# Two attention layers of a four-layer kernel, reordered as a two-step software pipeline

## The reference

```python
def nsa_attention(h, ...):                    # layer 3, 16 heads of 64 in 4 groups
    o_cmp = ...   # attention to 15 compressed blocks of 32 keys (a small MLP makes them)
    s_sel = einsum('bcgrd,bgckd->bcgrk', qc, kg) * scale + bias     # selected keys
    o_sel = softmax(s_sel) @ vg
    o_win = banded_attention(q, kwn, vwn, WIN - 1, 1, rel_bias)     # window of 256
    return (g0 * o_cmp + g1 * o_sel + g2 * o_win).reshape(B, S, D_MODEL) @ w_out

def dilated_attention(h, w_q, k_shared, v_shared, w_out, rel_bias): # layer 4
    q = (h @ w_q).reshape(B, S, N_DIL, N_KV, GQA_R, HEAD_DIM)       # 3 dilations
    for gi, (window, dilation) in enumerate(DILATIONS): ...         # (128,1) (512,4) (2048,16)
    o = sum over dilations of o_i * softmax(lse)_i                  # one joint softmax
    return o.reshape(B, S, D_MODEL) @ w_out
```

## Time and profile before

| | us |
|---|---|
| median of 3 runs | 1893.71 (1890.61 to 1898.06) |
| profiled execution | 1888.3, of which the span is 1886.5 |
| layer 3, from its first scores to the next stage's first matmul | 1104.25 to 1249.82 |
| layer 4, the same | 1516.11 to 1666.05 |
| TensorE in the span | busy 95%, mean granted clock 0.967 |

### The profile page before, as it was taken

How to read it: one execution, slowest core, us unless ns; L and a number is a source line. 1 busy time by engine, 2 the same in 40 slices (tenths; PEclk the granted TensorE clock), 3 DMA queues, 4 the chain that set the end, 5 groups by cost and what they waited for, 6 DMA issues and landing times.

```text
span 1886.5 us, 31683 instructions
## 1 busy us (share of the span) xinstructions
PE 1794.1 (95%) x13416; PEld 1684.9 (89%) x13416; DVE 1222.6 (65%) x1918; ACT 935.6 (50%) x1280; POOL 124.1 (7%) x35
## 2 busy tenths in 40 slices
PE   7999999999999999999999978799999988889998
PEld 6999999999889999999998877569998977779996
DVE  6976766877569767668775657556554734456453
ACT  5446565544355465655443546445443654445442
POOL 2612000000017120000000000000000000000000
PEclk9899999999999999999999999789999998899999
DMA  8684445555546644455555462224555645225552
GB/s 235 163 235 147 149 157 186 167 183 179 202 140 188 192 144 148 157 191 166 180 179 205 135 181 91 90 67 157 179 201 194 182 139 134 90 90 184 185 211 79
DMA packets 249148, 305.75 MB, mean 162 GB/s; under 512 B 9778, under 2 KB 224142, under 8 KB 249007
## 3 DMA queue, kind: packets, MB, share of 16 engines
q1 hardware_dynamic: 235959, 289.66, 47.7%
q10 hardware_dynamic: 13048, 14.07, 3.5%
HBM read 299.51 MB, written 4.19 MB: 161 GB/s over the span
## 4 chain that ended last, share of the span: by engine, by line
PE 76%; DVE 10%; DMA 6%; ACT 5%; issue 2%; DVEq 1%; ACTq 0%; SPq 0%
PE psum L463 23%; PE psum L464 23%; PE psum L465 23%; DVE wlo L439 3%; DMA raw<-in_b_w_q 2%; ACT whi L431 2%; DMA raw<-in_w_ffn_gate 2%; PE psum L2385 1%; DMA raw<-in_a_w_in 1%; DMA raw<-in_b_w_out 1%; ACT work L2018 1%; DVE work L2246 1%; DMA x<-in_x 1%; DMA raw<-in_a_w_out 1%; DVE hT L617 0%
## 5 line engine op out<-in xcount | busy, mean ns | idle before, releaser
L431 ACT ACTIVATE whi<-raw 128x2048 fp32r<-128x2048 f32 (+2 forms) x277 | 526.6, 1903 | 552.3 <-PE psum L465 177.6
L439 DVE TENSOR_TENSOR wlo<-raw,whi 128x2048 fp32r<-128x2048 f32 x249 | 563.3, 2281 | 183.3 <-PE psum L465 158.7
L463 PE MATMUL psum<-hT,whi 128*128 128x256 f32 x2160 | 616.9, 286 | 7.5 <-DVE wlo L439 3.8
L464 PE MATMUL psum<-hT,whi 128*128 128x256 f32 x2160 | 613.0, 284 | 0.0
L465 PE MATMUL psum<-hT,wlo 128*128 128x256 f32 x2160 | 612.9, 284 | 0.0
L463 PEld LDWEIGHTS psum<-hT,whi 128*128 128x128 f32 x2160 | 416.4, 193 | 10.9 <-issue 5.5
L464 PEld LDWEIGHTS psum<-hT,whi 128*128 128x128 f32 x2160 | 416.5, 193 | 0.1
L465 PEld LDWEIGHTS psum<-hT,wlo 128*128 128x128 f32 x2160 | 416.2, 193 | 0.0
L439 POOL TENSOR_TENSOR wlo<-raw,whi 128x2048 fp32r<-128x2048 f32 (+1 forms) x28 | 122.8, 4390 | 585.6 <-ACT whi L431 402.7
L463 PE MATMUL psum<-whi,hT 128*128 128x256 f32 (+2 forms) x448 | 145.1, 324 | 1.1 <-issue 1.1
L465 PE MATMUL psum<-whi,hT 128*128 128x256 f32 (+2 forms) x448 | 144.3, 322 | 0.0
(11 more groups left out here) (352 smaller groups left out, 2832.0 us busy)
## 6 DMA issues: line engine op xcount, KB each, us to landing
raw<-in_w_in SPq DMA_DIRECT2D x78, 1024.0 KB, 5.7
raw<-in_ffn_w_up SPq DMA_DIRECT2D x44, 1024.0 KB, 5.2
raw<-in_w_ffn_gate SPq DMA_DIRECT2D x22, 1024.0 KB, 5.4
raw<-in_w_ffn_up SPq DMA_DIRECT2D x22, 1024.0 KB, 6.4
raw<-in_w_ffn_down SPq DMA_DIRECT2D x22, 1024.0 KB, 5.0
raw<-in_ffn_w_down SPq DMA_DIRECT2D x22, 1024.0 KB, 5.2
raw<-in_b_w_q SPq DMA_DIRECT2D x12, 1024.0 KB, 5.7
raw<-in_a_w_in SPq DMA_DIRECT2D x10, 1024.0 KB, 5.8
```

The source lines that it names most:

```text
L431: act.activation(part(whi, n, HIGH_SLOTS), part(raw, n, RAW_SLOTS), ACT.Copy).then_inc(high_made, 1)
L439: eng.tensor_tensor(part(wlo, n, LOW_SLOTS), part(raw, n, RAW_SLOTS), part(whi, n, HIGH_SLOTS).bitcast(F32), ALU.subtract).then_inc(stream ...
L463: nc.tensor.matmul(dst, left[0], right[0], start=first, stop=False)
L464: nc.tensor.matmul(dst, left[0], right[1], start=False, stop=False)
```

## The change

Both loops are turned into a pipeline of two steps:

- TensorE issues `scores(s+1)` before `context(s-1)` and `turn(s)`, and waits with it for the maxima of step s (`maxima_ready`), no longer for the copies.
- The transposes have banks of their own: 6 and 7 in layer 3, one for each head. In layer 4 they are cut into pieces of up to 4 blocks (an even step 3 pieces, an odd one 2), which take banks 5 and 7 in turn; a piece waits for the copy of the piece before last.
- VectorE weighs step s and then finds the maxima of s+1, and does its other work after that. ScalarE does `exps(s)` and then `copies(s-1)`. Probabilities and sums are held twice.
- Layer 3 has only banks 4 and 5 left for context, so groups 0 and 1 are copied out (`take_group`), their compressed part goes to a bank of its own and is added (`sum_group`). Layer 4 has bank 6 left, of which VectorE copies each finished half out (`take_context`), and bank 4 for dense products.
- The table `FILL` places the dense halves. In layer 3 evictions and `make_high` come at other steps. In layer 4 `evict` stands at steps 4g and 4g+1 behind `copies(s-1)`, and at 4g+3 ahead of it; the steps of `make_lows` in the code are the same numbers.

```diff
-            FILL = {0: ((6, 0), (6, 1)), 1: ((7, 0), None), 2: ((7, 1), (8, 0)), 3: ((8, 1), None), 4: ((9, 0), None),
-                    5: ((9, 1), (10, 0)), 6: ((11, 0), None), 7: ((12, 0), (13, 0)), 8: ((14, 0), None), 9: ((14, 1), None)}
...
+            FILL = {0: ((6, 0), (6, 1)), 1: ((7, 0), (7, 1)), 2: ((8, 0), (8, 1)), 3: ((9, 0), None), 4: ((9, 1), None),
+                    5: ((10, 0), None), 6: ((11, 0), None), 7: ((12, 0), None), 8: ((13, 0), None), 9: ((14, 0), (14, 1))}
...
+                        if s:
+                            pe.wait_ge(turned_copied.sem, turned_copied.at(2 * s + e - 1))
...
+                scores(0)
                 for s in range(STEPS):
-                    scores(s)
                     fill(s, 0)
+                    if s + 1 < STEPS:
+                        scores(s + 1)
...
-                    copies(s)
-                    if s == 0:
+                    if s:
+                        copies(s - 1)
+                    if s == 1:
                         evict(6)
+                    if s == 2:
+                        evict(7)
...
+                        evict(9)
                         block_high(1)
-                        make_high(act, n0 + 10 + HIGH_SLOTS + 1)
-                    if s == 6:
-                        make_high(act, n0 + 11 + HIGH_SLOTS + 1)
+                    if s in (6, 7, 8, 9):
+                        make_high(act, n0 + s + 4 + HIGH_SLOTS + 1)
...
-                        make_high(act, n0 + 13 + HIGH_SLOTS + 1)
-                    if s == 8:
+                        take_group(0)
...
+                    if s == 10:
+                        evict(14)
...
-                    if s == 12:
+                    if s == 13:
...
+                def sum_group(g):
+                    p = GROUP_BLOCKS[g]
+                    dve.wait_ge(bank_full.sem, bank_full.at(p + 1))
+                    dve.wait_ge(group_taken.sem, group_taken.at(g + 1))
+                    dve.tensor_tensor(part[:, g, :], own(p), part[:, g, :], ALU.add).then_inc(group_summed.sem, 1)
+
+                maxima(0)
+                for s in range(STEPS):
+                    weigh(s)
+                    if s + 1 < STEPS:
+                        maxima(s + 1)
...
+            FILL = {}
+            for g in range(QUADS - 1):
+                a, b, c = ([(LEAD + ND * g + i, j) for j in range(2)] for i in range(ND))
+                FILL[4 * g - 1], FILL[4 * g] = (None, None, a[0]), (a[1], None, b[0])
+                FILL[4 * g + 1], FILL[4 * g + 2] = (b[1], None, c[0]), (None, c[1], None)
...
+            def turns(s):
+                _, t, _, _ = step(s)
+                if t:
+                    return (((0, 0), (0, 1), (0, 2), (0, 3)), ((0, 4), (0, 5), (1, 0), (1, 1)),
+                            ((1, 2), (1, 3), (1, 4), (1, 5)))
+                return ((0, 0), (0, 1), (0, 2)), ((1, 0), (1, 1), (1, 2))
...
+            def turn_bank(m):
+                return bank((5, 7)[m % 2])
...
             def own(n):
-                return bank(4 + n % 2)
+                return bank(4 + n % 2) if n < LEAD else bank(4)
...
-                            pe.wait_ge(bank_free.sem, bank_free.at(n - 1))
+                            pe.wait_ge(bank_free.sem, bank_free.at(n if n >= LEAD else n - 1))
...
-                        pe.wait_ge(turned_copied.sem, turned_copied.at(2 * s))
+                        pe.wait_ge(maxima_ready.sem, maxima_ready.at(2 * s))
...
+                    for m, blocks in enumerate(turns(s), turns_until(s)):
+                        if m >= 2:
+                            pe.wait_ge(turned_copied.sem, turned_copied.at(m - 1))
+                        pe.wait_ge(probs_ready.sem, probs_ready.at(2 * s + blocks[-1][0] + 1))
+                        for i, (e, n) in enumerate(blocks):
+                            mm = nc.tensor.transpose(turn_bank(m)[:, i * P:(i + 1) * P],
+                                                     probs[:, 2 * (s % 2) + e, n * P:(n + 1) * P], ident)
                         mm.then_inc(probs_turned.sem, 1)
...
-                    pe.wait_ge(turned_copied.sem, turned_copied.at(2 * s + 2))
-                    if t and j >= 2:
-                        pe.wait_ge(parts_ready.sem, parts_ready.at(j - 1))
-                    b = bank(6 + j % 2)
+                    pe.wait_ge(turned_copied.sem, turned_copied.at(turns_until(s + 1)))
+                    if t and j:
+                        pe.wait_ge(context_taken.sem, context_taken.at(j))
+                    b = bank(6)[:, (j % 2) * S:(j % 2 + 1) * S]
...
+                scores(0)
+                fill(-1, 2)
                 for s in range(STEPS):
-                    scores(s)
-                    if i < 2 * count:
-                        dense_half(i)
-                        i += 1
+                    fill(s, 0)
+                    if s + 1 < STEPS:
+                        scores(s + 1)
+                    fill(s, 1)
                     if s:
                         context(s - 1)
                     turn(s)
-                    if s % 2 == 0 and i < 2 * count:
-                        dense_half(i)
-                        i += 1
+                    fill(s, 2)
...
                 def copies(s):
-                    _, _, _, blocks = step(s)
-                    for e in range(2):
-                        act.wait_ge(probs_turned.sem, probs_turned.at(2 * s + e + 1))
-                        act.activation(sbuf_t[:, 2 * (s % 2) + e, 0:blocks * P], slot(e)[:, 0:blocks * P], ACT.Copy) \
+                    for m, blocks in enumerate(turns(s), turns_until(s)):
+                        e, n = blocks[0]
+                        at, wide = 768 * e + n * P, len(blocks) * P
+                        act.wait_ge(probs_turned.sem, probs_turned.at(m + 1))
+                        act.activation(turned_probs[s % 2][:, at:at + wide], turn_bank(m)[:, 0:wide], ACT.Copy) \
                            .then_inc(turned_copied.sem, 1)
...
                     exps(s)
-                    if u < count and i >= 2:
-                        evict(u + i - 1)
-                    if s and s % 2 == 0:
-                        high(s // 2 - 1)
-                    copies(s)
-                    if u < count and i == 0:
-                        evict(u)
+                    if u < count and i == 3:
+                        evict(u + 2)
+                    if s:
+                        copies(s - 1)
+                    if u < count and i < 2:
+                        evict(u + i)
+                    if s >= 4 and s % 2 == 0:
+                        high(s // 2 - 2)
+                copies(STEPS - 1)
+                high(STEPS // 2 - 2)
                 high(STEPS // 2 - 1)
...
+                def take_context(j):
+                    dve.wait_ge(context_ready.sem, context_ready.at(j + 1))
+                    dve.tensor_copy(context_rows[:, j % 2, :], bank(6)[:, (j % 2) * S:(j % 2 + 1) * S]) \
+                       .then_inc(context_taken.sem, 1)
...
+                    weigh(s)
+                    if s + 1 < STEPS:
+                        maxima(s + 1)
                     if s and s % 2 == 0:
-                        low(s // 2 - 1)
+                        take_context(s // 2 - 1)
                     if s % 4 < 3:
                         make_lows(dve, n0 + min(LEAD + ND * (s // 4) + s % 4 + 2, count + 2))
+                    if s >= 4 and s % 2 == 0:
+                        low(s // 2 - 2)
+                low(STEPS // 2 - 2)
                 low(STEPS // 2 - 1)
```

More of the change, by code:

```diff
@@ L1939, in context @@
                     g = j // 2
-                    b = bank(4 + g)[:, (j % 2) * S + t * P:(j % 2) * S + (t + 1) * P]
+                    if g >= 2 and s % 4 == 0:
+                        pe.wait_ge(group_taken.sem, group_taken.at(g - 1))
+                    b = bank(4 + g % 2)[:, (j % 2) * S + t * P:(j % 2) * S + (t + 1) * P]
+                    last = g < 2 and s % 4 == 3
                     for n in range(2 * (t + 1)):
@@ L1970, in _ @@
                         turn_blocks(0)
-                    if s == 15:
-                        block_context(0)
-                        block_context(1)
+                block_context(0)
+                block_context(1)
                 context(STEPS - 1)
@@ L2228, in _, with maxima @@
                 dve.wait_ge(table_load.sem, table_load.at(16 * (P // ROWS + 2)))
-                for s in range(STEPS):
+                def maxima(s):
                     j, t, keys = step(s)
@@ L2287, in _ @@
                             block_weights(t_)
+                for g in range(2):
+                    sum_group(g)
                 for c in range(GROUPS):
                     dve.wait_ge(context_read.sem, context_read.at(c + 1))
-                    dve.tensor_tensor(hT[1][:, 2 * c:2 * c + 2, :].rearrange("p a s -> p (a s)"), bank(4 + c),
+                    dve.tensor_tensor(hT[1][:, 2 * c:2 * c + 2, :].rearrange("p a s -> p (a s)"),
```

(32 more changed lines are left out.)

185 lines of the change are left out of this document (113 added, 72 removed).

## The result

The changed kernel takes 1917.52 us (median of 4 runs, 1914.46 to 1923.52) against 1892.16 us (1887.38 to 1898.06, 4 runs, those shown ahead among them). The ratio is 1.0136, 95% interval 1.0098 to 1.0175. The profiled execution has a span of 1916.0 us, 29.5 more than before.

The account below looks back on a forecast made before the run. In layer 3 TensorE and VectorE, both loaded, wait for each other in turn; layer 4's middle rounds have little left to win. Layer 3 -25 and layer 4 +50 give +25 on the 1893.71 median: 1918 us, range 1885 to 1936.

Parts of the forecast that it names:

- Layer 3, -25: Layer 3 loop: scores no longer wait for the copies, 25 us saved, bounds -33 to -18.
- The cut parts: Layer 3's stretch to step 10 and its tail: 79 in place of 96.6 us, 37.5 in place of 48.97.
- Layer 4, +50: Layer 4 loop: a chain through all engines with bare loads makes it 50 us longer.
- the walk: Layer 4 chain priced leg by leg from the trace: 23.9, 20.9 and 12.2 us, +52 over the loop.
- The rounds: Layer 4's groups of four steps: first +16.6 us, next two +22.2 and +21.3, last -8.
- Stalls of third pieces: Layer 4, TensorE: transposes of an even step's third piece wait about 10 us for copies, twice a round.
- Load 5.1 us, nine bare: Layer 4: nine weight loads of 5.1 us each, from low part to split, covered by no other work.
- The clock: Layer 4, TensorE: half clock after two 10 us stalls costs 4.5 us a round; +40 without clock losses.
- The ring: Layer 4: low part, load, split, exponentials, copies and third piece wait on each other, 57.0 us a round at full clock.
- The rival that the loads are half hidden: Layer 4: loads end early or low parts come early, each of 9 legs loses 3 us; 1874 to 1894, chance 0.14.
- The other two: Pipeline works in both loops, 1854 us, chance 0.08; layer 3 gives back only 10, 1934 us, chance 0.12.
- rounds 2 and 3: Layer 4's two middle groups of four steps, 39.25 and 40.19 us before, said to have little left to win.

Follow-up runs that it names:

- both cuts: Two runs on the changed kernel: layer 4 low parts made a step or two earlier, 1844.28 us; layer 4 splits run a step later, behind the copies, 1853.95 us.
- the dose of half a load: Changed kernel with nine layer 4 weight loads bringing only half their unit (0.5 MB): 1909.48 us against 1921.94.
- early low parts: Layer 4 low parts made a step or more earlier: on the changed kernel 1844.28 us; on changed layer 3 with old layer 4, 1853.99 us.
- the longer filling: Changed kernel with 88 and 74 transposes of a constant ahead of third pieces in layer 4's three rounds: 1911.22 us.

## Why the prediction came out

The predicted 1918 us is 0.5 us from the median. The mechanism came out as walked, but so small a distance is luck. The two loops together grew by 31.5 us where +25 was forecast. Against that, 2 us less lie ahead of layer 3, and the kernel before was profiled in an execution 4 us below its median (1888.3 against 1892.16), while the changed one's profile (1917.9) lies at its median. Point by point:

- **Layer 3, -25**: -23.7. The cut parts came out at 80.6 us (79 walked) and 41.2 (37.5 walked, and 4 for the clock, which is at 0.79 there; no run prices that part). VectorE's waits ahead of the even maxima fell only from 22.0 to 14.9 us, where I had said under 8; of these 7.1 lie ahead of the first maxima, where the kernel before waits about as long (7.8; the one trace puts this wait down to a transfer, the other to the scores). Its waits for exponentials fell by 13.7 us (17.5 to 3.8), which the prediction did not count apart. The transposes' waits fell as said.
- **Layer 4, +50**: +55.2, against the +52 of the walk, which was rounded down. The rounds walked as 58.4, 61.5 and 61.5 took 59.6, 61.0 and 61.3; the last, walked as 21, took 23.3. Stalls of third pieces: 8.3 to 11.2 us, where 10 was said. The clock of the rounds is 0.77 to 0.81, under the 0.85 named.
- **Load 5.1 us, nine bare**: eight of the nine are between 4.8 and 5.2 us, one 6.4. The Trainium skill ("DMA: Bandwidth & Descriptors", section Measured) gives 6.15 us for 1 MB, measured on transfers issued from GpSimd; as an estimate the loop would be 9 us longer by it, and the trace does not have them.
- **The clock**: the walk has 2.3, 4.5 and 4.5 us in the three rounds, 11.3 in all; 10 to 12 measured. The rule of the Trainium skill that a loop whose waits idle TensorE falls back to the slow clock at each turn ("TensorE: Matmul & The Clock Gate", section "HAM oscillation — how this bites in real kernels") agrees with these rows: all six third pieces of the changed kernel came at half clock.
- **The ring as cause**: shown by both cuts and by the dose of half a load.
- The rival that the loads are half hidden was refuted by the 77.5 us of waits; VectorE had its spare time, but behind the waits. The other two fell with the loops, at -23.7 and +55.2 us.

What was missing in the prediction: it set the banks aside and gave their order no price. Of the 60.3 us of waits at the pieces, 46.5 go with the loads, and 13.8 stay. It did not see that moving three lines would open the ring. And it held that rounds 2 and 3 had little left to win: for the pipeline that is so (1.9 and 1.1 us over the old order, both with early low parts), but against the kernel before early low parts and pipeline together took 4.8 and 6.3 us off them (34.4 and 33.9 us in place of 39.3 and 40.2).

## What to carry to other kernels

When a pipeline gets one step deeper, list for each buffer which step gives it free and which step needs it full: here the activations moved a step apart, while the weights' low part, load and split stayed in one step, and the deeper order closed these into a ring through four engines. Such a ring is cheap to find (walk one round with prices from the trace) and to cut (three lines, 73 us). Expect the deeper pipeline to pay where nothing else fills the waits, as in the last four steps here. After the cut, small stalls that look fillable can be chains: see what else waits for the work that you move before counting its length as gain.

## What the runs showed of the hardware

A load of 1 MB takes 5.1 us from its release to the split behind it (median of nine), one of 0.5 MB 3.7 us: by these two, as an estimate, 2.2 us of it do not depend on the size.

Filling TensorE's idle time with 6 us of useless transposes and leaving 3 to 5 us empty did not keep its clock up (pieces at 1.11 us). Ahead of one piece, the fourth, 1.9 us were left, and it took 0.66 us. With the longer filling at most 1.7 us were left ahead of any piece, and all six took 0.66 us or less, at a mean granted clock of 0.97 against 0.79. The idle time just ahead does not decide by itself: in the changed kernel one `context` took 0.88 us after a wait of 2.81, and another, of the same twelve matmuls, 1.54 us after 2.47.
